# Attention in a hybrid trunk: the probabilities are divided by their sum before the transposes, one head on VectorE and one on GpSimd, and a latent item's maximum is taken in two parts

## The reference, cut to what matters

```
def gqa_attend(q, k, v):                       # branch A, 8 query heads, 2 key heads
    s = einsum('bqhgd,bkhd->bhgqk', q, k) * (dh ** -0.5)
    p = softmax(s, axis=-1)
    o = einsum('bhgqk,bkhd->bqhgd', p, v)

# branch B, 8 heads, for blocks of 128 latent queries
s_loc = einsum('bqhd,bqkhd->bhqk', qi, kg) * scale + rpb   # gathered window keys + bias
s_ctx = einsum('bqhd,bchd->bhqc', qi, kc) * scale
p = softmax(concatenate([s_loc, s_ctx], -1), -1)
o = p[..., :nk] @ vg + p[..., nk:] @ vc
```

## Time and profile before

| | |
|---|---|
| median of 3 runs | 2988.04 us (2988.01 to 2989.48) |
| profiled execution, its own time | 2993.4 us |
| its span | 2991.6 us |
| granted TensorE clock, mean | 0.986 |
| busy: PE, DVE, ACT, POOL | 2854.0, 1162.6, 1038.8, 1046.0 us |
| attention of layer 0 | 627.5 to 816.6 us of the span |
| attention of layer 1 | 2239.3 to 2378.9 us of the span |

### The profile page before, as it was taken

The page is one execution under the profiler, slowest core; times in us unless marked ns, Lnnn a source line. Parts: engine busy times, 40 slices in busy tenths (PEclk is TensorE's granted clock), DMA queues, the critical chain, the costliest instruction groups (busy, mean ns, idle before and its releaser), DMA issues.

```text
span 2991.6 us, 57456 instructions
## 1 busy us (share of the span) xinstructions
PE 2854.0 (95%) x24887; PEld 2452.8 (82%) x24887; DVE 1162.6 (39%) x1811; ACT 1038.8 (35%) x1779; POOL 1046.0 (35%) x721
## 2 busy tenths in 40 slices
PE   6998999988999999999999999899999999999999
PEld 5888888866788888899999878788787788878887
DVE  3854442345711123422222377444235722242223
ACT  4543222245622223422222265332226532333223
POOL 3335543302133332322222223455420344434443
PEclk8999999999999999999999999999999999999999
DMA  7224332200022232222222131322210034323332
GB/s 256 62 62 147 116 100 73 60 19 9 4 64 64 78 99 57 64 64 64 65 63 64 57 99 43 115 88 83 86 46 4 23 96 134 109 81 96 99 99 78
DMA packets 306027, 230.89 MB, mean 77 GB/s; under 512 B 25265, under 2 KB 277617, under 8 KB 304881
## 3 DMA queue, kind: packets, MB, share of 16 engines
q1 hardware_dynamic: 299152, 202.48, 22.7%
q0 software_dynamic: 3776, 17.91, 1.7%
q10 hardware_dynamic: 2848, 6.82, 0.6%
HBM read 216.17 MB, written 11.98 MB: 76 GB/s over the span
## 4 chain that ended last, share of the span: by engine, by line
PE 89%; DVE 4%; issue 2%; ACT 2%; DMA 1%; SPq 1%; POOL 1%; ACTq 0%; DVEq 0%; POOLq 0%
PE ps L484 20%; PE ps L486 20%; PE ps L485 20%; PE ps L642 6%; PE ps L596 3%; PE ps L617 2%; PE ps L634 2%; PE ps L523 1%; PE ps L972 1%; PE ps L500 1%; PE ps L950 1%; DVE stat L1813 1%; PE ps L502 1%; PE ps L922 1%; PE ps L501 1%
## 5 line engine op out<-in xcount | busy, mean ns | idle before, releaser
L2259 POOL TENSOR_TENSOR wl<-wring,wh 128x1024 fp32r<-128x1024 f32 (+1 forms) x310 | 720.6, 2326 | 1339.3 <-ACT wh L1338 1334.8
L484 PE MATMUL ps<-hh,wh 128*128 128x496 f32 (+2 forms) x2168 | 769.3, 355 | 6.9 <-DVE R L2106 3.5
L486 PE MATMUL ps<-hh,wl 128*128 128x496 f32 (+2 forms) x2168 | 758.9, 350 | 0.0
L485 PE MATMUL ps<-hl,wh 128*128 128x496 f32 (+2 forms) x2168 | 758.6, 350 | 0.0
L484 PEld LDWEIGHTS ps<-hh,wh 128*128 128x128 f32 x2168 | 408.7, 189 | 65.2 <-issue 6.3
L1338 ACT ACTIVATE wh<-wring 128x1024 fp32r<-128x1024 f32 (+1 forms) x310 | 305.8, 987 | 447.7 <-PE ps L486 424.4
L485 PEld LDWEIGHTS ps<-hl,wh 128*128 128x128 f32 x2168 | 409.1, 189 | 52.8 <-issue 3.4
L486 PEld LDWEIGHTS ps<-hh,wl 128*128 128x128 f32 x2168 | 408.5, 188 | 49.9
L484 PE MATMUL ps<-fh,wh 128*128 128x496 f32 (+2 forms) x744 | 262.8, 353 | 0.0
L486 PE MATMUL ps<-fh,wl 128*128 128x496 f32 (+2 forms) x744 | 262.8, 353 | 0.0
L485 PE MATMUL ps<-fl,wh 128*128 128x496 f32 (+2 forms) x744 | 262.8, 353 | 0.0
(11 more groups left out here) (321 smaller groups left out, 4347.2 us busy)
## 6 DMA issues: line engine op xcount, KB each, us to landing
wring<-in_w_ffn SPq DMA_DIRECT2D x128, 512.0 KB, 3.5
wring<-in_w_in SPq DMA_DIRECT2D x110, 512.0 KB, 3.6
wboth<-in_w_mod SPq DMA_DIRECT2D x80, 512.0 KB, 6.6
wring<-in_w_branch SPq DMA_DIRECT2D x32, 256.0 KB, 2.6
wring<-in_w_out SPq DMA_DIRECT2D x16, 512.0 KB, 4.0
x_store<-R POOLq DMA_DIRECT2D x2, 3072.0 KB, 9.0
R<-x_store POOLq DMA_DIRECT2D x2, 3072.0 KB, 11.0
wring<-in_w_in SPq DMA_DIRECT2D x16, 256.0 KB, 3.7
```

What stands on the lines that cost most here:

```text
L484: mm(ps[:, t0:t1], ahk, rh[:, k, t0:t1], start=(k == 0), stop=False)
L485: mm(ps[:, t0:t1], ahk, rl[:, k, t0:t1], start=False, stop=False)
L486: last = mm(ps[:, t0:t1], alk, rh[:, k, t0:t1], start=False, stop=(k == kn - 1))
L2259: G.tensor_tensor(slot_view(wl, n % NSPL, l, name, i), w, slot_view(wh, n % NSPL, l, name, i).bitcast(F32), ALU.subtract)\
```

## The change

PE no longer spreads the inverse sums: L622 and its wait go, as does ACT's copy of them (L1149). Instead the probabilities are divided before they are turned. In round p DVE waits for both exponentials of item p, takes the two reciprocals apart, and multiplies head 1's probabilities in place. POOL waits for the reciprocal of head 0 and multiplies head 0's. PE's transposes wait for these products instead of the exponentials. DVE's product of the output becomes a plain copy. In latent items of branch A, DVE takes the maximum over the 512 latent columns as soon as those scores are there, the maximum over the 256 context columns after that, and the smaller of the two negated values.

```diff
@@ tensor engine, attention
                         for c0, (n0, n1) in runs:
+                            if c0 and br == "A":
+                                last.then_inc(*pe_done.mark("S latents", l, p))
...
-                        pe.wait_ge(*dve_done.at("rsum", l, p - 2))
-                        for u in range(2):
-                            inv = stat[:, 2 * ((p - 2) % 4) + u, 1:2]
-                            last = mm(PS[3][HD * u:HD * u + HD, 512 + P:512 + 2 * P], inv.to_broadcast([P, HD]), ident,
-                                      start=True, stop=True)
                         last.then_inc(*pe_done.mark("O", l, p - 2))
...
-                            pe.wait_ge(*act_done.at("exp", l, p - 1, u))
+                            pe.wait_ge(*(dve_done if u else pool_done).at("prob", l, p - 1, u))
@@ scalar engine, attention_scalar
-                if p >= 2:
-                    eng.wait_ge(*pe_done.at("O", l, p - 2))
-                    nc.scalar.activation(orec[:, :], PS[3][:, 512 + P:512 + 2 * P], ACT.Copy)\
-                        .then_inc(*act_done.mark("rsums", l, p - 2))
@@ vector engine, attention
-                        dve.wait_ge(*pe_done.at("S", l, p))
+                        split = br == "A" and t < LT
+                        dve.wait_ge(*pe_done.at("S latents" if split else "S", l, p))
...
+                            if split:
+                                if u:
+                                    dve.wait_ge(*dve_done.at("max", l, p, 0))
+                                V.tensor_reduce(stat[:, sl, 0:1], ps[:, 0:LAT], AX.X, ALU.max, negate=True)
+                                dve.wait_ge(*pe_done.at("S", l, p))
+                                V.tensor_reduce(small[:, 57:58], ps[:, LAT:TOK], AX.X, ALU.max, negate=True)\
+                                    .then_inc(*dve_done.mark("max parts", l, p, u))
+                                dve.wait_ge(*dve_done.at("max parts", l, p, u))
+                                V.tensor_tensor(stat[:, sl, 0:1], stat[:, sl, 0:1], small[:, 57:58], ALU.min)\
+                                    .then_inc(*dve_done.mark("max", l, p, u))
+                                continue
...
-                    if 1 <= p <= len(work):
-                        sums = stat[:, 2 * ((p - 1) % 4):2 * ((p - 1) % 4) + 2, 1:2]
-                        dve.wait_ge(*act_done.at("exp", l, p - 1, 1))
-                        V.reciprocal(sums, sums).then_inc(*dve_done.mark("rsum", l, p - 1))
+                        for u in range(2):
+                            total = stat[:, 2 * (p % 4) + u, 1:2]
+                            dve.wait_ge(*act_done.at("exp", l, p, u))
+                            V.reciprocal(total, total).then_inc(*dve_done.mark("inverse", l, p, u))
+                        dve.wait_ge(*dve_done.at("inverse", l, p, 1))
+                        pr = prob[br][p % 2][:, 1, 0:n]
+                        V.tensor_scalar(pr, pr, total, None, ALU.mult).then_inc(*dve_done.mark("prob", l, p, 1))
                     if p >= 2:
...
-                        V.tensor_tensor(o, ps, inv, ALU.mult).then_inc(*dve_done.mark("o", l, p - 2))
+                        V.tensor_copy(o, ps).then_inc(*dve_done.mark("o", l, p - 2))
@@ gpsimd, at the end of each round p of the attention loop, behind the bias work
+                    n = key_tiles(br, t) * P
+                    pool.wait_ge(*dve_done.at("inverse", l, p, 0))
+                    pr = prob[br][p % 2][:, 0, 0:n]
+                    G.tensor_tensor(pr, pr, stat[:, 2 * (p % 4), 1:2].to_broadcast([P, n]), ALU.mult)\
+                        .then_inc(*pool_done.mark("prob", l, p, 0))
```

More of the change, by code:

```diff
@@ L225, in program @@
         mrow = sb("mrow", [P, P])
-        orec = mrow
         tiles = ([4, 5, 0, 1, 2, 3], [5, 4, 3, 2, 1, 0])
@@ L616, in attention @@
                                 c0 = HD * (u if br == "A" else 2 * hp + u)
-                                mm(PS[3][HD * u:HD * u + HD, 512:512 + P], vt[b][:, c0:c0 + HD],
-                                   probT[br][:, u, b, :], start=(b == 0), stop=(b == nk - 1))
-                        pe.wait_ge(*dve_done.at("rsum", l, p - 2))
-                        for u in range(2):
-                            inv = stat[:, 2 * ((p - 2) % 4) + u, 1:2]
-                            last = mm(PS[3][HD * u:HD * u + HD, 512 + P:512 + 2 * P], inv.to_broadcast([P, HD]), ident,
-                                      start=True, stop=True)
+                                last = mm(PS[3][HD * u:HD * u + HD, 512:512 + P], vt[b][:, c0:c0 + HD],
+                                          probT[br][:, u, b, :], start=(b == 0), stop=(b == nk - 1))
                         last.then_inc(*pe_done.mark("O", l, p - 2))
@@ L1812, in attention @@
                                 dve.wait_ge(*dve_done.at("bias", l, p, u))
+                            if split:
[9 more added lines that the diff above has]
+                                continue
                             V.tensor_reduce(stat[:, sl, 0:1], ps[:, 0:n], AX.X, ALU.max, negate=True)\
                                 .then_inc(*dve_done.mark("max", l, p, u))
-                    if 1 <= p <= len(work):
-                        sums = stat[:, 2 * ((p - 1) % 4):2 * ((p - 1) % 4) + 2, 1:2]
-                        dve.wait_ge(*act_done.at("exp", l, p - 1, 1))
-                        V.reciprocal(sums, sums).then_inc(*dve_done.mark("rsum", l, p - 1))
+                        for u in range(2):
[5 more added lines that the diff above has]
+                        V.tensor_scalar(pr, pr, total, None, ALU.mult).then_inc(*dve_done.mark("prob", l, p, 1))
                     if p >= 2:
                         br, hp, t = work[p - 2]
-                        dve.wait_ge(*act_done.at("rsums", l, p - 2))
-                        ps, inv = PS[3][:, 512:512 + P], orec[:, :]
+                        dve.wait_ge(*pe_done.at("O", l, p - 2))
+                        ps = PS[3][:, 512:512 + P]
                         o = (oA if br == "A" else oB)[:, hp, t * P:t * P + P]
@@ L1825, in attention @@
                             o = by_window(oB[:, hp, 0:LAT])[:, 2 * t:2 * t + 2, :, :]
-                            ps, inv = (v.rearrange("p (g r c) -> p g r c", g=2, r=8) for v in (ps, inv))
-                        V.tensor_tensor(o, ps, inv, ALU.mult).then_inc(*dve_done.mark("o", l, p - 2))
+                            ps = ps.rearrange("p (g r c) -> p g r c", g=2, r=8)
+                        V.tensor_copy(o, ps).then_inc(*dve_done.mark("o", l, p - 2))
                     if 1 <= p <= len(work):
```

## The result

The changed kernel took 3065.25 us (median of 6 runs, 3055.54 to 3069.15), the kernel before beside it 2987.27 us (6 runs, 2979.41 to 2989.48). The ratio is 1.0256, with a 95% interval of 1.0243 to 1.027: 76 us slower. The forecast was 3060, that is +72.

The account below looks back on a forecast made before the run. PE was taken to bound attention, in branch A level with the chain through the exponential. Terms 11.5 + 10.2 + 21.6 + 30 = 73.3, less 1 to 2, gave 72 on the median 2988.04: 3060; 8-in-10 range 3030 to 3088.

Parts of the forecast that it names:

- DVE's own round: Attention items: DVE's work plus one ScalarE exponential of standing still becomes the period, 5.35 in A and 4.68 in B.
- Branch A, +10.2 and +11.5 forecast: Attention branch A: latent items go from 4.63 to 5.35; +10.2 us in layer 0, +11.5 in layer 1.
- Branch B, +30 and +21.6 forecast: Attention branch B: latent items go from 3.33 to 4.68; +30 us in layer 0, +21.6 in layer 1.
- POOL has some 3 us free per item: Branch B: bias loads and sums now precede POOL's product, but POOL was said to have this much time free.
- The exclusion: Attention products: DVE's ends 0.42 (0.27 for 512 columns) after POOL's; without exclusion the sum is some 7 us less.
- The change of branches: From A to B: a 256-column POOL product adds about 1 us a layer, first items save more; together -1 to -2.
- PE stays the bound, faster: Rival, attention: DVE's waits are met on arrival, PE saves 0.32 per item; 2962 us, chance 0.04.
- Milder: Rival, attention: no exclusion, a cheap minimum, exponentials found done; 3015 to 3045 us, chance 0.14.
- The clock falls as well: Rival, branch B: PE's holes lower the clock, +18 to +73; with slow POOL product 3072 to 3100, chance 0.20.
- POOL's lower bound of 1.2: POOL's product of 768 columns in attention: lowest price by slope without surcharge, against some 1.47 expected and 1.8 at most.

Follow-up runs that it names:

- e5: Kernel before, with only DVE's reciprocal of item p taken in round p instead of p+1, so DVE waits for the exponential: 3027.15 us, 1.0136 of before.
- e7: Changed kernel with both heads' products on DVE and none on POOL: 3049.87 us, 1.0227 of before.
- e3: Changed kernel with both heads' products on POOL, DVE keeping reciprocals and waits: 3018.31 us, 1.0116 of before.
- e4: Changed kernel with six idle matmuls on PE behind the scores of each branch B item from the second on: 3060.05 us, 1.0253 of before.
- e1: Changed kernel with the maximum of branch A latent items taken in one piece again: 3050.71 us, 1.0238 of before.
- e2: Changed kernel with DVE's two reciprocals and product moved behind its copies of the output and turned probabilities: 3029.73 us, 1.0157 of before.
- e8: e2 with the maximum of branch A latent items taken in one piece: 3021.78 us, 1.0124 of the kernel before.

## Why the prediction was right

**The mechanism.** The prediction said that DVE's own round, one exponential of standing still included, becomes the period. The profile shows it (the earlier trace rows against the timeline of A above: a hole of 0.99 ahead of the reciprocal, PE released by DVE's copy), and four runs test it: the wait alone costs 41 us (e5), work put inside the wait is free (e7), work taken from behind it is worth 42 us (e3), and 39.5 us more of PE cost nothing (e4).

**How close, and how much of it is luck.** The route was right; that the whole is off by 4 us (76 against 72) is in part luck. The forecast was 6.5 us too high in branch A and 8.0 us too low in branch B, and the two errors nearly cancel. The next paragraphs take them one by one.

**Branch A, +10.2 and +11.5 forecast, +8.2 and +7.0 measured.** Both maxima were known 2.45 after the first began (2.51 forecast), the product ended at 4.48 (4.6), the period was 5.21 (5.35). The minimum of one column took 0.16 (0.15). The whole shortfall of layer 1, 4.5 us, is more than 16 x 0.14 = 2.2. The rest is in the first two items, which took 9.44 us (2268.50 to 2277.94) against 10.41 before, where the forecast had 2 x 0.72 more. In e4, whose branch A is the same code, they took 10.64, with a stretch at the lower clock; the changed kernel's profile shows none there (1.00). So 1.2 us of this shortfall are the clock's, which the forecast did not have in branch A.

**Branch B, +30 and +21.6 forecast, +33.3 and +26.3 measured.** An item beside POOL's product alone took 4.60 (4.68 forecast). Two things are missing from the forecast. The first is behind its sentence that POOL has some 3 us free per item: true of POOL, which was late with its product at the change of branches alone, but its bias sums lie in that free time, and one that runs when DVE's product comes shuts it out. The product takes up to 0.96 instead of 0.49, and such items take 5.08. The second is the clock. In e4, where it hardly falls, branch B is 30.2 and 25.2 us longer than before: in layer 0 nearly the whole difference to the forecast (33.3 against 30) is the clock's, in layer 1 only 1.0 us is, and six items of 5.07 to 5.17 instead of 4.60 make 2.9 of the other 3.6. In layer 0 a block of six items of B, 26.2 in the forecast, took 26.96 (769.42 to 796.38) and the next one 28.06 (to 824.44), with one item of 6.56 at the lower clock; it was 18.71 in the earlier trace rows. In e4 both took 26.95. Groups by shape of the changed kernel, layer 0:

```profile
L2495 POOL TENSOR_TENSOR R<-R,stat 128x512 f32<-128x512 f32 x16 | 16.7, 1041 | 39.4 <-DVE stat L1823 39.4
L1823 DVE RECIPROCAL stat<-stat 128x1 f32<-128x1 f32 x96 | 15.4, 161 | 53.2 <-ACT R L1133 53.2
L1826 DVE TENSOR_SCALAR R<-R,stat 128x512 f32<-128x512 f32 x16 | 10.4, 653 | 0.6
```

POOL's product took 1.041 for 512 columns and 1.47 for 768, as read off (1.04 and 1.47). DVE's took 0.78 for 768 columns, ending 0.41 after POOL's (0.42 forecast), and 0.653 in the mean for 512. The second line is the cost in one number: in layer 0 DVE stood 53.2 us in front of its reciprocals, more than the 41.6 that the stage became longer. PE lost its two sum products per item at the same time, which gains nothing where PE isn't the bound: six more matmuls cost nothing either (e4).

**The exclusion.** The prediction placed DVE's product 0.42 behind POOL's end, from the earlier trace rows. Measured: 0.41 in the changed kernel (669.44 to 669.85), 0.41 in e1 (2309.40 to 2309.81), 0.42 in e2 (671.82 to 672.24), whatever the length of the meeting. The Trainium skill ("SBUF — State Buffer", "Who interferes with whom") states that a DVE instruction in a 2-port mode and a GpSimd instruction cannot use the port pair that the two engines share at the same time: the one that issues first has it for its whole length, and the other waits. The traces agree, with DVE's product at 0.62 alone and up to 1.86 beside a product of POOL that had started 0.03 before it. Leaving the exclusion out would have made the forecast 7 us lower, and its length in another order is where the expectations of e2 and e8 went wrong.

**The change of branches.** POOL's product there stands behind memsets and bias sums, and PE's transposes wait for it. In the kernel before, PE waited 3.93 one item later. Changed kernel, then kernel before, both in layer 0:

```profile
744.44 1.12 PE L630 MATMUL ps<-cst,R 128*128 128x128 f32 x4 [5.09 <-POOL R L2495]
```

```profile
739.02 1.12 PE L617 MATMUL ps<-R 128*64 128x128 f32 x8 [3.93 <-DVE R L1834]
```

From the first scores of B to the second it takes 7.86 (737.63 to 745.49) against 2.46 before, and from the second to the third 4.54 against 8.43. The two together are 1.5 us longer in layer 0 and 2.2 in layer 1 (13.75 against 11.55). The forecast had 2 x 1.35 for them as for all latent items of B, less 1 to 2 for both layers together, so this term was right.

**The rivals.** *PE stays the bound, faster* is refuted by e4 and by the holes. *Milder* needed no exclusion and found exponentials; neither was so. *The clock falls as well* was half right: branch B of layer 0 was granted a clock of 0.88 and that of layer 1 0.92, against 0.96 and 0.97 before. Two stretches of the changed kernel, 5 us each, in branch B of layer 0 (columns as above):

```profile
775.00:780.00 5.00, 4.24 (x24) 2.97 (x24) 4.03 (x11) 1.94 (x5) 3.17 (x5) 0.66 0.08 20
785.00:790.00 5.00, 2.75 (x28) 2.04 (x28) 3.98 (x12) 1.99 (x5) 2.04 (x3) 1.00 0.00 0
```

In the first the clock is partly at the 1.2 GHz level and PE is busy 4.24 of 5.00 us, with most of its holes filled by slower matmuls; in the second it is at 2.4 GHz, with 2.75. Single items got much longer under the lower clock, up to 6.56 us (the rival had 6.2); but most of the slow time fell into holes that PE had anyway, and a long item was followed by a short one (6.51 and then 4.19 from 2384.31 on), so that the price was some 4 us (e4) and not the rival's 18 to 73.

**Slips in the working.** Branch B has 24 items in layer 0 and 16 in layer 1, 40 and not 48; the rival's 18 to 73 should read 15 to 61. The stage of layer 0 was said to become about 211 us; 189.1 + 10.2 + 30 is 229, and it took 230.6. POOL's lower bound of 1.2 by the slope of the earlier trace rows comes out as 1.28. None of them enters the sum of the forecast.

## What to carry to other kernels

An in-order engine that is busy 65% of a stage can still be its bound: add up its round with the waits in it, and look where a new wait stands before what work it adds. Here work placed inside a wait was free, and work behind it, even half a microsecond, was paid at every item. When two engines exclude each other, moving one of them moves the meeting too: price every order with the full length of both, and count the other engine's unrelated work as well.

## What the runs showed of the hardware

- An in-place product of DVE with a factor per partition took 0.62 us for 768 columns and 0.49 for 512 with no product or sum of POOL beside it. The one of 768 took 0.78 to 1.87 beside POOL's product and ended 0.41 to 0.42 after it in the changed kernel, e1 and e2, and 0.42 after in the earlier trace rows too, where POOL's instruction had another shape. The one of 512 ended 0.28 after the POOL instruction that it met, a product (e2) or a bias sum (changed kernel).
- The granted clock was 0.88 in branch B of layer 0, where PE stood still for 1.4 to 1.9 us at a time, and 0.97 in e4, where idle matmuls lay in these holes. In branch A it was 0.95 in layer 0 and 1.00 in layer 1, where the latent items do the same. What makes it fall was not tried.
- Code that is the same took 1412.4 us between the two attention stages in the changed kernel's profiled execution, 1422.7 in the one before and 1421.2 in that of e4. Nothing here says why, and it is the reason why the stages and not the spans were compared.
